# A transformer block on one core: the forget gates' logarithms at the ends of the first two pairs of heads, and a new order of the first units

## What is computed

```python
mod = c_act @ ada_w[l] + ada_b[l]                 # 9 vectors of 1024: shift, scale, gate x 3
h = modulate(rms_norm(x, norm_ffn1[l]), sh1, sc1)
x = x + 0.5 * g1 * swiglu(h, ffn1_w_gate[l], ffn1_w_up[l], ffn1_w_down[l])
...
log_f = jax.nn.log_sigmoid(fa + forget_b)         # branch a: 8 heads x 512 tokens
F = jnp.cumsum(log_f, axis=1)
s = q.k * scale + F[t] - F[s]                     # causal, then softmax, times v
...
s = q.k * scale + rel_bias[clip(t - s)]           # branch b: then softmax, times v
```

## Time and profile before

| | us |
|---|---|
| three runs, median (lowest to highest) | 1170.51 (1170.43 to 1171.03) |
| the profiled execution's own time | 1172.53 |
| its span, first to last instruction | 1170.8 |
| TensorE busy | 1154.2 |
| DVE busy | 625.7 |
| ACT busy | 451.4 |
| POOL busy | 59.1 |

### The profile page before, as it was taken

One profiled execution on the slowest core, in us unless ns is written; L12 is line 12 of the kernel. 1 busy time (PEld: TensorE's weight loads), 2 busy tenths in 40 slices (PEclk: granted clock), 3 DMA queues, 4 the chain that ended last, 5 costly groups with the idle time before them and its releaser, 6 DMA issues.

```text
span 1170.8 us, 16224 instructions
## 1 busy us (share of the span) xinstructions
PE 1154.2 (99%) x5734; PEld 977.2 (83%) x5734; DVE 625.7 (53%) x1052; ACT 451.4 (39%) x709; POOL 59.1 (5%) x86
## 2 busy tenths in 40 slices
PE   8999999999999998999999999999999999999998
PEld 7788888888888997888888888899888888888887
DVE  4766666666555666765555666756333333333332
ACT  4132232233222355655555666543332222322232
POOL 3301000000000000200000110000000000000000
PEclk9799999999999998999999999999999999999999
DMA  9567666556555413533244442241333333333331
GB/s 313 157 198 245 196 202 211 168 178 224 172 169 164 111 56 90 136 91 90 72 114 96 115 118 87 84 125 47 108 90 94 103 90 101 96 85 99 99 112 73
DMA packets 221149, 151.45 MB, mean 129 GB/s; under 512 B 5078, under 2 KB 202916, under 8 KB 221108
## 3 DMA queue, kind: packets, MB, share of 16 engines
q1 hardware_dynamic: 217108, 138.76, 39.4%
q0 software_dynamic: 3280, 9.79, 3.1%
q10 hardware_dynamic: 720, 2.36, 0.5%
HBM read 148.73 MB, written 4.52 MB: 131 GB/s over the span
## 4 chain that ended last, share of the span: by engine, by line
PE 93%; DVE 2%; issue 2%; DMA 1%; ACT 1%; ACTq 0%; DVEq 0%; POOLq 0%; POOL 0%; SPq 0%
PE bank L1489 28%; PE bank L1491 28%; PE bank L1490 28%; PE bank L1822 2%; PE bank L1838 1%; PE bank L1837 1%; PE bank L1815 1%; PE bank L1810 1%; DMA xin<-in_x_dram 1%; DMA raw<-in_ffn_w_gate_dram 1%; PE bank L1520 1%; DVE hL L1011 1%; PE bank L1616 0%; PE bank L1529 0%; DVE tmp L1006 0%
## 5 line engine op out<-in xcount | busy, mean ns | idle before, releaser
L1489 PE MATMUL bank<-hH,wH 128*128 128x512 f32 (+1 forms) x1072 | 414.3, 386 | 2.6 <-DVE hL L1011 2.2
L1490 PE MATMUL bank<-hL,wH 128*128 128x512 f32 (+1 forms) x1072 | 410.2, 383 | 0.0
L1491 PE MATMUL bank<-hH,wL 128*128 128x512 f32 (+1 forms) x1072 | 410.1, 383 | 0.0
L616 ACT ACTIVATE wH<-raw 128x1024 fp32r<-128x1024 f32 (+1 forms) x169 | 176.1, 1042 | 503.7 <-PE bank L1491 503.7
L945 DVE TENSOR_TENSOR wL<-raw,wH 128x1024 fp32r<-128x1024 f32 (+1 forms) x169 | 203.2, 1202 | 286.1 <-ACT wH L616 285.5
L1489 PEld LDWEIGHTS bank<-hH,wH 128*128 128x128 f32 x1072 | 202.6, 189 | 43.4 <-issue 4.4
L1491 PEld LDWEIGHTS bank<-hH,wL 128*128 128x128 f32 x1072 | 202.3, 189 | 39.5
L1490 PEld LDWEIGHTS bank<-hL,wH 128*128 128x128 f32 x1072 | 202.5, 189 | 38.3
L1489 PE MATMUL bank<-actH,wH 128*128 128x512 f32 (+1 forms) x332 | 126.9, 382 | 0.0
L1491 PE MATMUL bank<-actH,wL 128*128 128x512 f32 (+1 forms) x332 | 126.6, 381 | 0.0
L1490 PE MATMUL bank<-actL,wH 128*128 128x512 f32 (+1 forms) x332 | 126.6, 381 | 0.0
(11 more groups left out here) (204 smaller groups left out, 1200.3 us busy)
## 6 DMA issues: line engine op xcount, KB each, us to landing
adaw<-in_ada_w_dram SPq DMA_DIRECT2D x28, 1024.0 KB, 5.9
raw<-in_ffn_w_gate_dram SPq DMA_DIRECT2D x43, 512.0 KB, 3.7
raw<-in_ffn_w_up_dram SPq DMA_DIRECT2D x43, 512.0 KB, 3.7
raw<-in_mix_w_in_dram SPq DMA_DIRECT2D x41, 512.0 KB, 3.7
raw<-in_ffn_w_down_dram SPq DMA_DIRECT2D x32, 512.0 KB, 3.7
adas<-in_ada_w_dram SPq DMA_DIRECT2D x16, 512.0 KB, 8.0
raw<-in_ffn_w_down_dram SPq DMA_DIRECT2D x16, 384.0 KB, 3.4
raw<-in_mix_w_out_dram SPq DMA_DIRECT2D x8, 512.0 KB, 3.7
```

The lines of the kernel that those rows point to most:

```text
L616: nc.scalar.activation(wH[s][:, :n * P], raw[s][:, :n * P], ACT.Copy).then_inc(hi_done, 1)
L1489: T.matmul(o, a[0], b[0], start=start, stop=False)
L1490: T.matmul(o, a[0], b[1], start=False, stop=False)
L1491: return T.matmul(o, a[1], b[0], start=False, stop=stop)
```

## The change

It does four things.

- The forget gates on ACT: the first exponential and the logarithm (`forget_log`) go to the end of the first pair, the last exponential (`forget_exp`) to the end of the second. DVE's `forget_sums` goes from the end of the first pair to the end of the second.
- DVE's split of the weights of gate unit 4 in the first pair (`prep(u0, 10, i, k0 + 4)`) goes behind the biased scores.
- The rows of the first blocks: POOL takes 2, 2, 3, 3 (was 2 each), TensorE 2, 1, 1, 2 (was 2, 3, 1, 0), DVE 4, 5, 4, 3 (was 4, 3, 5, 6).
- TensorE's order in `first_units` is new, with 26 dummy products more; the dummies write the upper half of a bank.

The queue of POOL in the mixer, and who waits for what there, is not changed.

```diff
-    ROWS_P = 2
-    ROWS_PE = ((6, 7), (5, 6, 7), (7,), ())
+    ROWS_P = (2, 2, 3, 3)
+    ROWS_PE = ((6, 7), (7,), (7,), (6, 7))
     ROWS_V = [DT - len(rows) for rows in ROWS_PE]
...
-            def forget_exp():
+            def forget_log():
                 act.wait_ge(fa_act, 1)
                 nc.scalar.activation(fgate[:, 1, :], fgate[:, 0, :], ACT.Exp, scale=-1.0).then_inc(fa_act, 1)
-
-            def forget_logs():
-
                 act.wait_ge(fa_act, 2)
                 nc.scalar.activation(fgate[:, 2, :], fgate[:, 1, :], ACT.Ln, bias=1.0).then_inc(fa_act, 1)
+
+            def forget_exp():
                 act.wait_ge(fa_act, 3)
                 nc.scalar.activation(fgate[:, 4, :], fgate[:, 2, :], ACT.Exp, scale=-1.0).then_inc(fa_act, 1)
...
                         if made:
-                            forget_exp()
                             prep(u0, 10, i, k0 + 3)
                         act.wait_ge(unit_done, i * 10 + u0 + k0 + 3)
                         nc.scalar.activation(vT[:, :], bank[:, B_V if made else 0, :], ACT.Copy).then_inc(v_copied, 1)
-                        if made:
-                            forget_logs()
                         prep(u0, 10, i, k0 + 4)
...
                         out_hi(1)
+                        if first:
+                            (forget_log, forget_exp)[pp]()
...
                         prep(u0, 10, i, k0 + 3)
-                        prep(u0, 10, i, k0 + 4)
+                        if not made:
+                            prep(u0, 10, i, k0 + 4)
...
                         biased_scores(1)
+                        if made:
+                            prep(u0, 10, i, k0 + 4)
                         normalised(0)
...
-                        if made:
+                        if first and pp == 1:
                             forget_sums()
...
                 dummies(20)
                 tiles(0, 0)
+                first_parts(1)
                 tiles(1, 0)
-                first_parts(1)
+                dummies(10)
                 first_sums(1)
                 tiles(2, 0)
                 tiles(3, 0)
                 tiles(0, 1)
                 tiles(1, 1)
+                first_parts(2)
                 tiles(2, 1)
-                first_parts(2)
+                tiles(3, 1)
                 first_sums(2)
-                tiles(3, 1)
+                first_parts(3)
+                dummies(10, B_ADA_START[3])
                 tiles(0, 2)
                 tiles(1, 2)
+                tiles(2, 2)
                 first_sums(3)
-                tiles(2, 2)
                 tiles(3, 2)
+                dummies(6, B_ADA_START[2])
```

More of the change, by code:

```diff
@@ L97, in hybrid_block @@
     AC, AC2 = 512, 512
-    ROWS_P = 2
-    ROWS_PE = ((6, 7), (5, 6, 7), (7,), ())
+    ROWS_P = (2, 2, 3, 3)
+    ROWS_PE = ((6, 7), (7,), (7,), (6, 7))
     ROWS_V = [DT - len(rows) for rows in ROWS_PE]
+    STEPS_P = [sum(2 * r - 1 for r in ROWS_P[:b]) for b in range(ADA0 + 1)]
+    STEPS_V = [sum(v - r for r, v in zip(ROWS_P[:b], ROWS_V)) for b in range(ADA0 + 1)]
     N_FIRST = 4
@@ L504, in first_rows @@
                 nc.gpsimd.tensor_scalar(adasp[:, b, :], adas[:, b, 0, :], csilu[:, 0:1], None, ALU.mult).then_inc(adasp_step, 1)
-                for k in range(1, ROWS_P):
+                for k in range(1, ROWS_P[b]):
                     scaled = sqx[:, 0:AC] if k % 2 else sqx[:, AC:]
-                    pool.wait_ge(adasp_step, (b * ROWS_P + k) * 2 - 1 - b)
+                    pool.wait_ge(adasp_step, STEPS_P[b] + 2 * k - 1)
                     nc.gpsimd.tensor_scalar(scaled, adas[:, b, k, :], csilu[:, k:k + 1], None, ALU.mult).then_inc(adasp_step, 1)
-                    pool.wait_ge(adasp_step, (b * ROWS_P + k) * 2 - b)
+                    pool.wait_ge(adasp_step, STEPS_P[b] + 2 * k)
                     nc.gpsimd.tensor_tensor(adasp[:, b, :], scaled, adasp[:, b, :], ALU.add).then_inc(adasp_step, 1)
@@ L1023, in normed @@
                     if b in (1, 2):
-                        first_rows(b, ROWS_P, ROWS_V[b])
+                        first_rows(b, ROWS_P[b], ROWS_V[b])
                     if b == 1:
@@ L1028, in normed @@
                     if b == 2:
-                        first_rows(3, ROWS_P, 4)
+                        first_rows(3, ROWS_P[3], 4)
                     if b == 3:
@@ L1072, in first_rows @@
                 acc = bank[:, B_ACC, :]
-                done = sum(n - ROWS_P for n in ROWS_V[:b])
                 for k in range(k0, k1):
@@ L1077, in first_rows @@
                     out = adasc[:, b, :] if k == ROWS_V[b] - 1 else acc
-                    if k > ROWS_P or b:
-                        dve.wait_ge(adas_step, done + k - ROWS_P)
-                    if k == ROWS_P:
+                    if k > ROWS_P[b] or b:
+                        dve.wait_ge(adas_step, STEPS_V[b] + k - ROWS_P[b])
+                    if k == ROWS_P[b]:
                         ins = V.tensor_scalar(out, adas[:, b, k, :], csilu[:, k:k + 1], None, ALU.mult)
@@ L1440, in _ @@
             mean_squares(0, slice(0, TT))
-            first_rows(0, ROWS_P, 4)
+            first_rows(0, ROWS_P[0], 4)
             normed()
@@ L1515, in first_sums @@
                     if n == 0:
-                        pe.wait_ge(adasp_step, (b + 1) * (2 * ROWS_P - 1))
+                        pe.wait_ge(adasp_step, STEPS_P[b + 1])
                     if n == AC // P:
-                        pe.wait_ge(adas_step, sum(n_v - ROWS_P for n_v in ROWS_V[:b + 1]))
+                        pe.wait_ge(adas_step, STEPS_V[b + 1])
                     cols = slice(n % (AC // P) * P, (n % (AC // P) + 1) * P)
@@ L1611, in last_sums, with dummies @@
                 return ins
-            def dummies(n):
+            def dummies(n, b=B_IDLE):
                 for _ in range(n):
-                    T.matmul(bank[:, B_IDLE, 0:2 * P], ident[:, :].bitcast(BF16)[:, 0:P], ident[:, :].bitcast(BF16), start=True, stop=True)
+                    T.matmul(bank[:, b, 2 * P:], ident[:, :].bitcast(BF16)[:, 0:P], ident[:, :].bitcast(BF16), start=True, stop=True)
             def spread():
```

## The result

| | us |
|---|---|
| kernel before, median of five runs (lowest to highest) | 1170.43 (1169.76 to 1171.03) |
| changed kernel, median of five runs | 1175.82 (1175.57 to 1177.44) |
| ratio, with its 95% interval | 1.0052 (1.0039 to 1.0065) |
| profiled execution after, its span | 1176.15, 1174.5 |

The change makes the kernel 5.4 us slower, which is 0.5%. One more run of the kernel before, beside e5 to e8, took 2345.64 us where the other 77 beside the experiments took 1168.1 to 1175.1, and is left out of every number.

The account below looks back on a forecast made before the run. TensorE was taken as the bound, busy 1154.2 of 1170.8 us. First pair -6.1, new wait +9.9 and start -0.5 gave +3.3 on the 1170.5 median: 1173.8 us, own range 1171.0 to 1176.4, over the cases 1170.6 to 1176.6.

Parts of the forecast that it names:

- The three terms: The first pair's gain, the new wait's loss and the start's gain: -6.1 + 9.9 - 0.5 = +3.3 us.
- the last one: Final step: the profiled execution stands 2.0 us over the median, and +3.3 is carried to the median, giving 1173.8.
- The first pair, -6.1: Mixer's first pair: TensorE's wait of 3.22 us and 2.84 us of slow clock go; low end 3.2.
- Steps moved for nothing: ACT's and DVE's forget steps at their new places behind the first two pairs cost TensorE nothing.
- The new wait, +9.9: Third pair: TensorE waits 7.1 us for POOL's late mask, plus 2.8 of slow clock; ends 7.0 and 10.4.
- The start, -0.5: First blocks: new rows and order gain 0.5 us, between a gain of 1.5 and a loss of 2.2.
- the high end: Start: POOL's addition falls beside DVE's `hL` of the third block, 1.0 us more.
- the start loses: Rival, chance 0.10: clock stays low at the start and POOL's addition hits DVE; +2.2 instead of -0.5, 1176.5 us.
- Nearly even: Rival, chance 0.13: third pair's wait at its low end of 7.0, as transfers land faster; +0.4, 1170.9 us.
- faster: Rival, chance 0.12: third pair's mask is not late, so only -6.6 is left, 1163.9 us.
- The table load: Rival, chance 0.03: the load ahead of the first pair's softmax still holds the exponentials; 3.2 of gain left, 1176.7 us.

Follow-up runs that it names:

- e5: e3_after_pool with the fourth block's narrow products left to DVE and 30 dummies instead of 10; 1167.59 us, ratio 0.9968.
- e8: e3_after_pool with POOL's third rows taken back, so two rows in each of the four blocks; 1167.22 us, ratio 0.9970.
- e2_start_only: The changed kernel's start with the mixer of before; 1172.65 us, ratio 1.0023 against the kernel before.
- e11_forget_first_pair: The changed kernel with all forget steps behind the first pair; 1170.43 us, ratio 1.0001 against the kernel before.
- e4_mixer_pool: e1_mixer_only with POOL's fetch of the third pair's bias moved ahead of the wait for the forget sums; 1165.16 us, ratio 0.9957.
- e3_after_pool: The changed kernel with POOL's fetch of the third pair's bias moved ahead of the wait for the forget sums; 1168.6 us, ratio 0.9986.
- e1_mixer_only: The kernel before with only the mixer's part of the change, the start untouched; 1174.4 us, ratio 1.0038.
- e9_sums_early: e8 with TensorE's sums of the fourth block back ahead of the six wide products of `tiles(2, 2)`; 1165.75 us, ratio 0.9962.
- e12_before_pool_line: The kernel before with only POOL's fetch of the third pair's bias moved ahead of the wait for the forget sums; 1170.78 us, ratio 1.0004.
- e7_narrow_more_wide: e3_after_pool with 30 dummies instead of 10 behind the narrow products, which stay; 1169.93 us, ratio 0.9993.

## Why the prediction was right, and where it was not

The direction and the mechanism were right: slower, by a new wait in the third pair. 1173.8 was forecast and 1175.8 measured, inside the range. That the spans of the two profiles differ by 3.7 where the sum says 3.3 is in part luck: the new wait was taken 1.1 too long and the start 0.9 too good, and these nearly cancel. The three terms as measured add up to 3.1, so that 0.6 lies elsewhere in the program. The steps that failed are the start's term and the last one, that the difference of the profiled executions can be carried to the median.

**The first pair, -6.1.** From S to the first product with v it took 454.95 - 57.44 = 397.51 us before and takes 449.28 - 57.88 = 391.40 now: -6.1. The table load ahead of the softmax (438.76, 1.28 us, with the exponential at 440.06) was not in the way. The Trainium skill's drain on top of a load (ScalarE: Activation LUTs, section What ACT_TABLE_LOAD costs) is not in this trace either: 438.76 + 1.28 is 440.04, and the exponential starts at 440.06. The load itself starts right behind a rounding of weights that ends at 438.75, so the drain is not in front of it either (timeline of ACT in the changed kernel):

```profile
437.69 1.06 ACT L618 ACTIVATE wH<-raw 128x1024 fp32r<-128x1024 f32 x1
438.76 1.28 ACT L813 ACT_TABLE_LOAD   x1
440.06 0.72 ACT L813 ACTIVATE prob<-prob,negmax 128x512 f32<-128x512 f32 x1
```

**That this is the gain of the median: wrong.** 2.8 of the 6.1 are slow clock, and e2_start_only shows that an execution can have the wait without it. The 77 runs of the kernel before that stand beside the twelve let one guess how common that is. They fall into groups by their mean granted clock:

| mean clock of the run | runs | median us (lowest to highest) |
|---|---|---|
| 0.994 and more | 37 | 1169.0 (1168.1 to 1170.2) |
| 0.991 to 0.993 | 29 | 1170.7 (1169.8 to 1172.3) |
| 0.988 to 0.990 | 11 | 1173.3 (1172.6 to 1175.1) |

The profiled execution, at 0.988, is of the last group. It had slow stretches at the start and in the first pair, and the gain of 6.1 was read from it; by their clock most runs have fewer, and so less to gain. That is argued and not shown: the runs without a profile don't say which stretch was slow. The changed kernel's profiled execution lies only 0.3 us over its median, the one of before 2.1 over its own: that is 1.8 of the 2.0 us by which the forecast is low.

**Steps moved for nothing: right.** Exponential, load and logarithm end at 460.92, and ACT's next weights, at 461.35, still wait 0.43 us for TensorE. DVE's weights behind the second pair's sums cost nothing either: none of TensorE's waits is for them. e11_forget_first_pair puts a price on the cover: one load and one exponential more behind the same pair, and TensorE waits 1.45 us.

**The new wait, +9.9: right in kind, 1.1 too long.** 5.99 for 7.1, since the `biasA` transfers took 6.52 us to land and not 7.74. The slow clock, 6.62 - 3.84 = 2.78, was as forecast. Together 8.8. It came from POOL's order, as the prediction said: one line of it takes the wait away. DVE's wait is 6.40 for the 7 that were to show it.

**The start, -0.5: wrong.** In the pair of profiles it is +0.4 (57.44 to 57.88, outside the 55.9 to 57.5 that were to show it). By the runs it is more: 2.7 us in e2_start_only (1.5 to 3.7) and 3.4 between e4_mixer_pool and e3_after_pool, both over the bound of 2.2 that I had set, though the interval of the first reaches below it. Three things are in it. Ahead of the third block's sums the order may gain: they start at 41.81 instead of 42.62, with six wide products more ahead of them, where 1.3 was forecast. That gain is not shown apart from the landing of the block, since the four profiles with the old start have them at 40.84 to 43.12 and those with the new one at 41.32 to 43.96. Behind them the clock falls, and stays low to about 49.5 in the changed kernel's profile and to 53.1 in e2_start_only and e3_after_pool, as the rival had it. That it falls there was taken from one row; with the old start it fell behind these sums in three profiles and not in the fourth (e1_mixer_only). POOL's addition hits `hL` and makes the pair 1.0 us longer, as stood only in the high end. The Trainium skill (GPSIMD Engine Reference, section Key points) says that POOL shares its SBUF interfaces with DVE and contends with DVE's instructions on two SBUF inputs, and 2.43 against 1.41 us agrees. How much of the 1.0 reaches S is not shown. And one step I did not take at all: that the fourth block's sums move behind six wide products. I had costed them as ready early and not asked who covers the 5.3 us from them to the last slices; that is the 1.5 us of e9_sums_early. The rival *the start loses* is therefore true as well, beside the forecast: its 2.2 us are nearer to what the runs give than the 0.5 gained.

**The rivals.** *Nearly even* and *faster* did not come; *faster* is what e3_after_pool makes of the change by one line, at 1168.6 instead of the 1163.9 that stood there, since the start's loss stays and the first pair's gain was taken from the slow profile. That rival was to decide at 515.68 - 504.25 = 11.4 us (the prediction has 11.3); the way from the running sum to the mask took 17.7. The table load did not hold the first pair.

## What to carry to other kernels

When a step moves to a later place, look for every wait on its semaphore, and for what stands behind that wait in the same in-order queue. Here a transfer that had nothing to do with the forget gates was held up with it, and putting it ahead turned +5.4 into -1.3 us against the kernel before. A profile is one execution: when it shows slow stretches of the clock, compare its own time with the median before counting all of them as gain. And when sums or columns are moved back behind other work, count what is left to cover the chain that starts from them.

## What was unexpected in the hardware

- The same wait of 3.22 us on TensorE was followed by 1.2 GHz in two profiled executions (the kernel before, and e12_before_pool_line, 6.65 us to the values) and by 2.4 GHz in one (e2_start_only, 3.90 us). One and the same program, the kernel before, takes 1168.1 to 1175.1 us, and the longer times go with a lower mean granted clock.
- The sixteen narrow products in a row of the new start were followed by 1.2 GHz where 10 dummies stood behind them (e3_after_pool and e8_pool_two_rows among others) and by 2.4 GHz where 30 did (e7_narrow_more_wide). The same start stayed at 1.2 GHz until 49.5 us in two profiles and until 53.1 in two others. The old start's twelve were followed by 1.2 GHz in three profiles and by 2.4 in one.
- Under contention both sides pay: DVE's pair of `hL` goes from 1.41 to 2.43 us, POOL's addition from 1.26 to 1.73 (the changed kernel's at 43.30 and 46.30).
